# Bias and state space parameter transfers moved to another queue, GpSimd's chunk work in three pieces, and a compact retention scan

## The reference

```python
def step(s, u_n):
    return g_chunk * s + u_n, s          # s is 64 x 64 for a head
_, s_prev = lax.scan(step, s0, moveaxis(u, 2, 0))
o_cross = einsum('bhnid,hi,bhnde->bhnie', qc, wq, s_prev)
return o_inner + o_cross                 # once forward, once on flipped tokens
```

## Time and profile before

| | |
|---|---|
| median of 3 runs | 4352.18 us |
| the profiled execution | 4353.51 us |
| its span, from which all rows are | 4351.7 us |
| its mean granted TensorE clock | 0.904 of 2.4 GHz |
| TensorE busy | 3602.3 us (83%) |
| VectorE, ScalarE, GpSimd busy | 2035.0, 1248.2, 1394.0 us |
| HBM traffic | 67 GB/s over the span |

### The profile page before, as it was taken

The page is one execution under the profiler, slowest core; times in us unless marked ns, Lnnn a source line. Parts: engine busy times, 40 slices in busy tenths (PEclk is TensorE's granted clock), DMA queues, the critical chain, the costliest instruction groups (busy, mean ns, idle before and its releaser), DMA issues. The chain is left out here.

```text
span 4351.7 us, 50216 instructions
## 1 busy us (share of the span) xinstructions
PE 3602.3 (83%) x19160; PEld 2784.5 (64%) x19160; DVE 2035.0 (47%) x3980; ACT 1248.2 (29%) x2762; POOL 1394.0 (32%) x660
## 2 busy tenths in 40 slices
PE   1888989999999684874866499999997559999995
PEld 1666766777777464663653277788875147678873
DVE  2175445555546633295231335555444335555534
ACT  3233334444444323101120212144321031133321
POOL 0246556333333152470543022211135212211243
PEclk6899999999999686997888799999998879999997
DMA  4201111121111032332225410000013531010122
GB/s 109 48 27 54 49 51 54 44 77 39 40 42 35 17 116 98 115 117 68 92 92 171 123 30 25 22 24 24 25 68 122 178 90 30 25 29 25 30 73 102
DMA packets 296747, 282.95 MB, mean 65 GB/s; under 512 B 65373, under 2 KB 260369, under 8 KB 294466
## 3 DMA queue, kind: packets, MB, share of 16 engines
q1 hardware_dynamic: 167040, 138.43, 10.7%
q10 hardware_dynamic: 129482, 141.43, 10.3%
HBM read 247.61 MB, written 43.80 MB: 67 GB/s over the span
## 5 line engine op out<-in xcount | busy, mean ns | idle before, releaser
L1586 POOL TENSOR_TENSOR w_hi<-w_raw,one 128x1024 fp32r<-128x1024 f32 x264 | 561.8, 2128 | 2809.8 <-PE psum L845 1389.2
L1589 POOL TENSOR_TENSOR w_lo<-w_raw,w_hi 128x1024 fp32r<-128x1024 f32 x264 | 673.2, 2550 | 20.7
L1698 PE MATMUL psum<-act_hi,w_hi 128*128 128x512 f32 x1280 | 512.3, 400 | 118.0 <-ACTq L1950 78.5
L845 PE MATMUL psum<-act_hi,w_hi 128*128 128x512 f32 (+1 forms) x1376 | 518.8, 377 | 12.3 <-DVEq L179 12.3
L845 PE MATMUL psum<-act_lo,w_hi 128*128 128x512 f32 (+1 forms) x1376 | 519.1, 377 | 0.0
L1698 PE MATMUL psum<-act_lo,w_hi 128*128 128x512 f32 x1280 | 517.3, 404 | 0.0
L845 PE MATMUL psum<-act_hi,w_lo 128*128 128x512 f32 (+1 forms) x1376 | 516.1, 375 | 0.0
L1698 PE MATMUL psum<-act_hi,w_lo 128*128 128x512 f32 x1280 | 508.7, 397 | 0.0
L321 PE MATMUL psum<-w_hi,act_hi 128*128 128x512 f32 x928 | 309.4, 416 | 164.0 <-DVE act_lo L346 46.8
L1698 PEld LDWEIGHTS psum<-act_hi,w_hi 128*128 128x128 f32 x1280 | 244.3, 191 | 173.1 <-issue 119.6
L321 PEld LDWEIGHTS psum<-w_hi,act_hi 128*128 128x128 f32 x928 | 179.4, 199 | 223.5 <-issue 76.4
(11 more groups left out here) (330 smaller groups left out, 5540.6 us busy)
## 6 DMA issues: line engine op xcount, KB each, us to landing
w_raw<-in_attn_w_in SPq DMA_DIRECT2D x80, 512.0 KB, 3.7
w_raw<-in_w_in SPq DMA_DIRECT2D x64, 512.0 KB, 4.0
arena<-x ACTq DMA_DIRECT2D x48, 512.0 KB, 4.3
arena<-in_w_mod ACTq DMA_DIRECT2D x16, 1536.0 KB, 6.2
w_raw<-in_w_out SPq DMA_DIRECT2D x40, 512.0 KB, 3.5
w_raw<-in_ssm_w_in SPq DMA_DIRECT2D x32, 512.0 KB, 3.6
x<-arena ACTq DMA_DIRECT2D x24, 512.0 KB, 2.9
arena<-in_x ACTq DMA_DIRECT2D x16, 512.0 KB, 5.3
```

Source lines behind the costliest of these rows:

```text
L845: ins = nc.tensor.matmul(psum[:, n % 2, 0:c], w[:, slot % 2, k * P:(k + 1) * P], a[:, k, c0:c0 + c], start=(m == 0), stop=(m == 23))
L1586: G.tensor_tensor(w_hi[:, par], w_raw[:, par], one[:, 0:1].to_broadcast([P, 1024]), ALU.mult).then_inc(slot_hi, 1)
L1589: G.tensor_tensor(w_lo[:, par], w_raw[:, par], w_hi[:, par].bitcast(F32), ALU.subtract).then_inc(slot_split, 1)
L1698: ins = nc.tensor.matmul(psum[:, h % 2, :], w[:, (3 + j) % 2, k * P:(k + 1) * P], a[:, k, c:c + 512], start=(m == 0), stop=(m == 23))
```

## The change

1. The skewing of the bias and the 14 parameter loads leave ScalarE's program. SyncE issues them between weight slots. The small tables of the bias move to another part of the arena, so that the parameters may land in stage 1. ScalarE waits for the bias only ahead of its first bias load. The load of `ident` counts on `const_loaded` in place of `k_load`.
2. GpSimd's `chunk` becomes `chunk_b`, `chunk_c_re` and `chunk_c_im`, each after another slot's split. `diagonal(c)` comes one slot later.
3. The scan's states become 128 x 64 (`SFC`), without the zero blocks: one scan instruction a step and direction instead of two, and four matmuls of 64 x 64 weights instead of two of 128 x 128. The product into `TMP` moves up ahead of the wait for the transposed keys.

```diff
-K_LOADS = 15
+K_LOADS = 14
@@ retention
-        SFB = region(20480, 2, NC, P)
+        SFC = region(20480, 2, NC, 64)
@@ mix_pe, out_of(n)
-                    nc.tensor.matmul(o, SFB[:, 0, n], tv[:, n * P:(n + 1) * P], start=True, stop=False, skip_group_check=True)
-                    nc.tensor.matmul(o, SFB[:, 1, n], TMP[:, n * P:(n + 1) * P], start=False, stop=False, skip_group_check=True)
+                    for d, v in enumerate((tv, TMP)):
+                        for h in range(2):
+                            nc.tensor.matmul(o[HALF[h]], SFC[HALF[h], d, n], v[HALF[h], n * P:(n + 1) * P],
+                                             start=(d == 0), stop=False, skip_group_check=True)
@@ mix_dve, ret_segment
                 dve.wait_ge(r_exp, 9 * it + 9)
+                rl(V.tensor_tensor(per(TMP), per(tq), wide(WQ[:, 1]), ALU.mult))
                 dve.wait_ge(r_kt, it + 1)
...
                 V.tensor_tensor(per(tv), per(tq), wide(WQ[:, 0]), ALU.mult)
-                rl(V.tensor_tensor(per(TMP), per(tq), wide(WQ[:, 1]), ALU.mult))
...
-                        for h in range(2):
-                            c = slice(64 * h, 64 * h + 64)
-                            ins = V.scalar_tensor_tensor(SFB[HALF[h], d, nxt, c], SFB[HALF[h], d, now, c],
-                                                         GC[HALF[h], d:d + 1], u[HALF[h]], ALU.mult, ALU.add)
+                        ins = V.scalar_tensor_tensor(SFC[:, d, nxt], SFC[:, d, now], GC[:, d:d + 1], u, ALU.mult, ALU.add)
@@ block.sync
+            def spread_bias():
+                sp.wait_ge(b_copied, 3)
+                sp.dma_start(bias_rows, spread[0:16].rearrange("p a b -> p (a b)")).then_inc(b_stored, 16)
+                sp.wait_ge(b_stored, 16)
+                for g in range(2):
...
+                    sp.dma_start(bias_mat[:, :, 256 * g:256 * (g + 1)], src).then_inc(b_skewed, 16)
...
+                sp.dma_start(bias_mat2, src).then_inc(b_skewed, 16)
             w1 = io["attn_w_in"][0]
-            for j in (7, 8, 9):
+            for j in (7, 8):
                 load_t((3 + j) % 2, j - 7, w1, slot_col(HALF_OF[j], 0))
-            with sp.Fori(1, HP) as hp1:
+            spread_bias()
+            load_t(0, 2, w1, slot_col(HALF_OF[9], 0))
+            load_a(0)
+            load_a(1)
+            for j in range(L1_PER_HP):
+                load_t((3 + j) % 2, 3 + j, w1, slot_col(HALF_OF[j], 0) + (0 if j < 7 else P))
+                if j in (0, 1):
+                    load_c(j)
+                if 1 <= j < 5:
+                    load_b((j - 1) % 2, (j - 1) // 2)
+            with sp.Fori(2, HP) as hp1:
@@ block.gpsimd
                 if n == 11:
-                    chunk(0)
+                    chunk_b(0)
+                if n == 12:
+                    chunk_c_re(0)
+                if n == 13:
+                    chunk_c_im(0)
                 for c in range(N_CHUNKS):
-                    if n == FIRST_SLOT[c] + 1:
+                    more = c + 1 < N_CHUNKS
+                    if n == FIRST_SLOT[c] + 1 and more:
+                        chunk_b(c + 1)
+                    if n == FIRST_SLOT[c] + 2:
                         diagonal(c)
-                        if c + 1 < N_CHUNKS:
-                            chunk(c + 1)
+                        if more:
+                            chunk_c_re(c + 1)
+                    if n == FIRST_SLOT[c] + 3 and more:
+                        chunk_c_im(c + 1)
@@ block.scalar
             t_act(act, 0, NT, t_src_rows(x_in, False), True, T_GAIN, 0)
-            act.wait_ge(b_copied, 3)
-            act.wait_ge(b_copied, 3)
-            act.dma_start(bias_rows, spread[0:16].rearrange("p a b -> p (a b)")).then_inc(b_stored, 16)
...
-            act.wait_ge(b_skewed, 48)
             stage_end(act, 1)
-            for g2 in range(2):
-                for i, name in enumerate(("ssm_a_re", "ssm_a_im")):
...
             act.sem_inc(g_evac[0], 1)
...
+            act.wait_ge(b_skewed, 48)
             for g in ORDER:
                 load_bias(0, g)
```

More of the change, by code:

```diff
@@ L127 @@
 T_DONE, F_DONE, Y_DONE = 2 * NT, 2 * NT, KT
-CONST_DONE, FC_DONE = 4, 2
+CONST_DONE, FC_DONE = 5, 2
 U_DONE, VT_DONE = 3 * NT * HP, 6 * HP
@@ L611, in evac_qkv @@
             return nc.scalar.activation(dst, src, ACT.Copy, scale=SCALE if p % 3 == 0 else 1.0)
-        onehot = region(0, 1152)
-        relb = region(1152, 16)
-        spread = region(1200, 3, 384)
+        onehot = region(20480, 1152)
+        relb = region(21632, 16)
+        spread = region(21648, 3, 384)
+        halves = lambda g2: slice(64 * g2, 64 * g2 + 64)
         c_cols = sb("c_cols", [P, KT, 2])
@@ L1234, in ret_segment @@
                 dve.wait_ge(r_exp, 9 * it + 9)
+                per = lambda v: v[:, 0:P * chunks(l)].rearrange("p (n c) -> p n c", c=P)
+                wide = lambda w: w.rearrange("p (o c) -> p o c", o=1).to_broadcast([P, chunks(l), P])
+                rl(V.tensor_tensor(per(TMP), per(tq), wide(WQ[:, 1]), ALU.mult))
                 dve.wait_ge(r_kt, it + 1)
@@ L1394, in mix_dve @@
             decays(0)
-            rl(V.memset(SFB[:, :, :, :], 0.0))
+            rl(V.memset(SFC[:, :, :, :], 0.0))
             own(V.memset(QBD[0][:, :, :], 0.0))
@@ new lines, in load_a, with load_c @@
+            def load_a(g2):
+                for i, name in enumerate(("ssm_a_re", "ssm_a_im")):
+                    src = io[name][0].rearrange("(gp g) p -> g p gp", g=2)[g2]
+                    sp.dma_start(KA[halves(g2), i], src, **slow).then_inc(k_load, 16)
+                dt = io["ssm_log_dt"][0]
+                sp.dma_start(KA[halves(g2), 2], bass.AP(tensor=dt.tensor, offset=dt.offset + g2, ap=[[0, 64], [2, 32]]),
+                             **slow).then_inc(k_load, 16)
+            def load_c(g2):
+                for i, name in enumerate(("ssm_c_re", "ssm_c_im")):
+                    src = io[name][0].rearrange("(q g) c p -> (g c) q p", g=8)
+                    sp.dma_start(KCL[:, i, :, 64 * g2:64 * g2 + 64], src).then_inc(k_load, 16)
@@ L1547, in _, with load_b @@
+            def load_b(i, g2):
+                src = io[("ssm_b_re", "ssm_b_im")[i]][0].rearrange("(gp g) p c -> g p gp c", g=2)[g2]
+                sp.dma_start(KB[halves(g2), i], src).then_inc(k_load, 16)
             w1 = io["attn_w_in"][0]
-            for j in (7, 8, 9):
+            for j in (7, 8):
                 load_t((3 + j) % 2, j - 7, w1, slot_col(HALF_OF[j], 0))
-            with sp.Fori(1, HP) as hp1:
+            spread_bias()
+            load_t(0, 2, w1, slot_col(HALF_OF[9], 0))
@@ L1612, in inputs_scaled, with each, power, chunk_b @@
                 link(G.tensor_tensor(KBB[:, 1], KBB[:, 1], tmp, ALU.add))
[L1614 to L1622, removed]
+            def each(v, c, n):
+                return v[:, 4 * c:4 * c + 4].rearrange("p g (o c) -> p g o c", o=1).to_broadcast([P, 4, n, 16])
+            def power(i, c, n):
+                return KP[:, i, 0:n, 4 * c:4 * c + 4].rearrange("p s (g o) -> p g s o", o=1).to_broadcast([P, 4, n, 16])
+            def chunk_b(c):
                 tmp8 = KTMP[:, 0:512].rearrange("p (g s c) -> p g s c", g=4, s=8)
@@ L1628, in chunk, with chunk_c_re @@
                         pool.wait_ge(k_bt, 2 * (c - 1) + ri + 1)
-                    link(G.tensor_tensor(dst, each(KBB[:, ri], 8), power(0, 8), ALU.mult))
-                    link(G.tensor_tensor(tmp8, each(KBB[:, 1 - ri], 8), power(1, 8), ALU.mult))
+                    link(G.tensor_tensor(dst, each(KBB[:, ri], c, 8), power(0, c, 8), ALU.mult))
+                    link(G.tensor_tensor(tmp8, each(KBB[:, 1 - ri], c, 8), power(1, c, 8), ALU.mult))
                     G.tensor_tensor(dst, dst, tmp8, ALU.subtract if ri == 0 else ALU.add).then_inc(k_b, 1)
                     pool.wait_ge(k_b, 2 * c + ri + 1)
-                tmp9 = KTMP.rearrange("p (g s c) -> p g s c", g=4, s=9)
-                cr, ci = (KCP[:, ri].rearrange("p g (t c) -> p g t c", c=16) for ri in range(2))
+            tmp9 = KTMP.rearrange("p (g s c) -> p g s c", g=4, s=9)
+            cr, ci = (KCP[:, ri].rearrange("p g (t c) -> p g t c", c=16) for ri in range(2))
+            def chunk_c_re(c):
                 if c == 0:
@@ L1639, in chunk, with chunk_c_im @@
                     pool.wait_ge(k_cst, 32 * c)
-                link(G.tensor_tensor(cr, each(KC[:, 0], 9), power(0, 9), ALU.mult))
-                link(G.tensor_tensor(tmp9, each(KC[:, 1], 9), power(1, 9), ALU.mult))
+                link(G.tensor_tensor(cr, each(KC[:, 0], c, 9), power(0, c, 9), ALU.mult))
+                link(G.tensor_tensor(tmp9, each(KC[:, 1], c, 9), power(1, c, 9), ALU.mult))
                 link(G.tensor_tensor(cr, cr, tmp9, ALU.subtract))
-                link(G.tensor_tensor(ci, each(KC[:, 0], 9), power(1, 9), ALU.mult))
+            def chunk_c_im(c):
+                link(G.tensor_tensor(ci, each(KC[:, 0], c, 9), power(1, c, 9), ALU.mult))
                 link(G.tensor_scalar(ci, ci, -1.0, None, ALU.mult))
```

(2 more changed lines are left out.)

31 lines of the change are left out of this document (6 added, 25 removed).

## The result

The changed kernel takes 4202.04 us (median of 4 runs, 4200.45 to 4205.34), the kernel before 4352.22 beside it (4352.09 to 4353.13). The ratio is 0.9654, with an interval of 0.9640 to 0.9667: 150 us less, where 168 were forecast. 4202 lies in the range, which the rivals had widened to 4215; it lies 18 us above the forecast itself and 1 us inside the forecast's own end, 4203. The terms of the sum missed by unequal amounts, and part 3's excess covers 4 us of what the other two lack.

| term | forecast | between the two traces | part alone (medians) |
|---|---|---|---|
| 1, transfers on SyncE | 72 | 62.8 | 61.9 |
| 2, chunk work in pieces | 56 | 43.2 | 45.5 |
| 3, scan | 40 | 44.2 | 41.9 |
| sum | 168 | 150.2 | 149.3 |

The account below looks back on a forecast made before the run. TensorE, busy 83% of the span, was taken to bound the kernel through its waits. 72 (transfers) + 56 (chunk pieces) + 40 (scan) = 168 us off 4352.2 gives 4184; range 4158 to 4215, own ends 4165 to 4203.

Parts of the forecast that it names:

- Stalls behind log_dt: SyncE's queue: two 17 us stalls at about 40 to 75 us; slot 3 lands near 79, covered by 5 us.
- rival (a): SyncE's queue: each narrow transfer stalls it, b loads about 21 us each, TensorE stands 25 us; 4212, chance 0.12.
- Part 2: Attention stage: 7 stalls of 8.2 us, less 0.6 each that stays, give 53; with 3 from pair 0, 56 us.
- Rival (c): Attention pairs: the pieces still cost, as VectorE slowed beside GpSimd holds up units; half the gain stays, 4210, chance 0.07.
- Pair 0: First head pair: looser order of chunk 0 and parameter products while VectorE is densest, worth 3 us (0 to 8).
- Part 3: Second block's scan: 29.3 us of waits and 14.7 for the lowered clock go, less charges of 1.5 and 2.5; 40 us.
- charge of 2.5 for the matmuls: TensorE's four narrow matmuls replacing two in 54 output chunks: +2.5 us taken, between -4 and +10.8.
- charge of 1.5 for the second layer: Second layer: idle time 2.9 us against a 3.4 us product, so keys come 0.5 us late in 3 segments.
- Rival (d): Scan: no shorter, as the instruction on 128 partitions takes twice as long; 42 us back, 4226, chance 0.03.
- (b): Four narrow matmuls: row tiles sharing one PSUM bank run one after another; 8 us on top, 4192, chance 0.14.
- Rival (e): Whole kernel: slower, as TensorE without its pauses is kept at 1.2 GHz; 4359 with 350 us there, chance 0.01.
- (f): First projection: starts late all the same, a slot or barrier hanging on SyncE's queue; 73 us back, 4257, chance 0.01.

Follow-up runs that it names:

- part alone: Each third of the change alone on the kernel before (4354.73 us): transfers 4292.85, chunk work in pieces 4309.21, scan 4312.80 us.
- cut chunks: Changed kernel with GpSimd's 13 operations of each of chunks 1 to 7 cut to a quarter of their columns; 4198.38 us.
- both other orders that were tried: On log_dt in rows: GpSimd's chunk 0 built one slot later, 4197.08 us; VectorE's four squarings spread over units 0, 2, 5, 7, 4203.17 us.
- three edits here: On log_dt in rows: chunk 0 one slot later 4197.08; squarings spread 4203.17; both plus one GpSimd operation less per chunk 4205.34 us.
- log_dt in rows: Changed kernel with log_dt loaded once, as one row of 64 values to each of 128 partitions, plus two small VectorE copies; 4199.81 us.

## Why the prediction was right, and where it was off

- **Start of stage 2**: right. 73.1 us against 72.9.
- **Stalls behind log_dt**: their cause, number and length were right (two of 16 to 18 us), and rival (a) is refuted: the b loads issue in 0.6 to 1.4 us. The step that failed is that "two stalls of 17 us fall at about 40 to 75 us" and slot 3 is "covered, by 5 us". They fell at 46 to 64 and 72 to 88, and slot 3 was to land near 79. In the second stall its DMA was in flight when the engines stood, so it landed with the stall's end and was split at 92.9. It also counted only SyncE's queue, although shows the DMA engines themselves idle, which stops ScalarE's bias loads and the evacuation behind them. Its 72 measured 62.8.
- **Part 2**: the waits for w_lo went as said, the pieces fit, chunks were in time. The term was mis-sized: 56 measured 43.2. The step that failed is "A part of the 8.2 may be VectorE slowed by GpSimd, which stays; that I put at 0.6 each". It allowed 4.2 us for 7 chunks. What stays in pairs 1 to 3 beyond TensorE's own work is 14.5 by the forecast's 3.2 a chunk. The two traces show what it is, to about 1 us: waits for ScalarE, 9.6 us in sum where the kernel before had 4.1, and four clock drops of 1.5 us. The cut chunks show 4.6 to 7.7 us of it to be VectorE slowed by GpSimd. The split of the old 34.2 us by two unknowns took all that wasn't TensorE's own for the stall's, the clock drops and the old waits for ScalarE too. Rival (c) named this mechanism with half of part 2; a quarter was lost.
- **Pair 0** gave 0.3 of 3: the wait in its third segment was 7.9 us before and is 9.0 now, behind VectorE's squarings and merges, and both other orders that were tried only moved it.
- **Part 3**: 40 against 41.9 alone and 44.2 between the spans. All of the 29.3 us went, with the 1.2 GHz stretch behind. The charge of 2.5 for the matmuls was wrong in sign: 54 times -0.05 is -3. The charge of 1.5 for the second layer can't be told apart in this term. Without the two charges the sum would be 44 + 3 = 47, so by the medians 5 us of it, by the means of what lies behind slot 54 4, are not accounted for. Rival (d) is refuted by 4.53 us, and (b), the rule of the Trainium skill ("TensorEngine Tiling (Array Packing)", Restrictions and Gotchas) that different row tiles can't use one PSUM bank at once, doesn't show in the time: in turn the four would take 0.84, by the forecast's estimate from L866, and they took 0.59.
- **Rival (e)**: refuted; the time fell, and the mean granted clock was 0.922, where the runs of the kernel before had 0.902 to 0.917. **(f)**: refuted by the 53.44.
- **The range**: the forecast's own lower end, 4165, doesn't follow from the terms named for it. 73 without the charge for tiles, 57 + 8 and 40 make 178, which is 4174.

What stays open: what causes the wait of 1.6 us early in each of pairs 1 to 3, why the clock drops behind the same wait in one profile and not in another, and whether shared 4-byte addresses or their closeness stalls the DMA engines.

## What to carry to other kernels

When transfers move from one queue to another, read the DMA engines' own idle slices: the stalls here held up SyncE's and ScalarE's queues alike, so cover has to be counted for all work that any queue feeds, not for the moved queue alone. When one engine's work is hidden beside another's, price how much it slows its neighbour before calling the rest of the time a stall. A change on a crowded path is judged where the path ends: three edits here were 4 to 10 us ahead of log_dt in rows alone at slot 13 and 1 to 2 us behind it at slot 24. And before a gain of a few us is put down to an edit, compare the granted clock in the same stretch of both traces: drops of 1.5 us each came and went here with edits that had no part in them.

## What the runs showed of the hardware

- A load whose 2048 pieces of 4 bytes read each of 32 addresses 64 times left all DMA engines idle for 16 to 18 us. The same load from 2048 different addresses did not, and 128 rows of 256 bytes from one address did not either.
- A scan instruction on 128 x 64 takes 275 ns in the median (108 times), one on 64 x 64 took 280 (216 times): twice the partitions cost nothing here.
- Beside GpSimd VectorE's small products are another matter. The third product of two squarings in pair 0 of the changed kernel, first on half the columns while GpSimd splits a slot, then alone:

```profile
234.13 2.44 DVE L2313 TENSOR_TENSOR arena<-arena 128x64 f32<-128x64 f32 x1
...
246.66 0.29 DVE L2313 TENSOR_TENSOR arena<-arena 128x128 f32<-128x128 f32 x1
```

- A head pair with the same instructions and the same waits lasts 167.5 or 170.6 us, with a granted clock of 1.00 or 0.98. Behind the same wait of 1.61 us the clock was 0.66 over 5 us in one profile and 1.00 in another.
